# Turning the mLSTM score tiles over, with keys on partitions, in a two-block kernel on one core

## The chip, the cores and the metric

One Trainium2 chip, one of its cores. The program computes two blocks of two layers each in float32, from inputs in HBM to one output of 1024 by 256. The metric is the device time of one execution in microseconds. The time before is 2889.97 us, the median of three runs (2889.78 to 2895.23).

## The reference, cut to what matters

The change lies in the mLSTM half of the even layer of the second block. There are 512 tokens (256 of context, then 256 latents), 4 heads of 128 channels, and two directions. In each direction a latent sees the whole context, and within its own stream what lies behind it in that direction. With one chunk in place of the chunks of 64 the sum over keys reads:

```
b      = cumsum(log_sigmoid(forget gate))            per head and direction
dlog   = b[t] - b[s] + li[s]                         for the keys s that t may see
m[t]   = max(state's own exponent (0 to begin with, decayed), max over s of dlog)
dw     = exp(dlog - m[t])
sc     = (q[t] . k[s]) * dw
h[t]   = (sum over s of sc * v[s]) / max(|sum over s of sc|, exp(-m[t]))
ml     = rmsnorm(sigmoid(o) * (h_forward + h_backward)) * ml_norm_g
gla    = rmsnorm(o_gla) * gla_norm_g * silu(gla_g)
y      = concat(gla, ml) @ even_w_out
```

## The kernel before

Five instruction streams are written out by hand: SP (the DMA queue), TensorE, VectorE, ScalarE and GpSimd. They meet at named semaphores, so the order within a stream is the order in the code. An `InOrder` wrapper puts a drain behind most VectorE and ScalarE instructions. The four PSUM banks `accs` are handed round by the projections (`ready` and `free` per bank), and the four banks `mix` are the scratch of everything else.

The even layer projects 14 weight panels of 256 columns (`G["even"]`, panels u = 0 to 13). Each weight is split in two parts (`high` by ScalarE, `low` by GpSimd, line 1451) and each product takes three passes (lines 697 to 699, function `split_half`, for features on partitions; lines 742, 743 and 749, function `kept_tokens`, for tokens on partitions). Panels 2 and 3 (GLA values) and 10 and 11 (mLSTM values) are by token; 12 and 13 are the mLSTM output gate and by feature. Between the halves of the panels run the steps of the GLA tree: event e = 2u + r on each engine (`even_after` on TensorE and ScalarE, `even_event` on VectorE), up to `gla_cross` (line 1093) and `gla_out` (lines 1105 to 1110). Until then the stream of projections sets the time and the tree fills in.

Then comes the part that is changed:

- `ml_select` (line 1136), on TensorE: 32 matmuls that lay the eight rows `li - b` (four heads, two directions) out over all 128 partitions, one bank at a time, with ScalarE copying each bank to `rall` (`gla_heads`, line 1760).
- Panel 13 (`even_last`), with the mean square and the root of the GLA heads between its halves (`head_mean_square` line 1148, `head_spread` line 1155).
- `mlstm`, in four passes p over the query blocks t = 2, 3, 0, 1 of 128 tokens. Queries lie on the partitions, keys on the free axis. On VectorE `decays(p)` adds the row `rall`, the column b[t] and a causal mask for eight (head, direction) rows (line 2622), takes the maximum along the keys (line 101), and ScalarE takes the exponential (lines 1793, 1796). VectorE then multiplies by the scores and sums along the keys (line 2663), divides by the denominator (lines 2673, 2676), TensorE transposes (line 1180), ScalarE copies to SBUF, TensorE multiplies by the values (line 1189), ScalarE copies out (`ml_h`).
- Gate and head norm by feature: `half_squares`, `head_root`, `head_reciprocal`, `normalise` (line 2642), once for the latents and once for the context.
- `even_out`: the output projection, 4 panels of 16 fp32 matmuls of 512 columns (line 1202 for the first, line 682 for the other three). Each stands as two instructions in the trace, as every fp32 matmul does.

The panel queue on SP loads a panel when the one four places earlier has been read. At panel 10 it also loads four causal masks (line 619).

## Time and profile before

| | us |
|---|---|
| median of three runs | 2889.97 |
| the profiled execution | 2889.35 |
| its span | 2887.4 |
| TensorE matmul busy | 2676.5 (93%) |
| VectorE busy | 1944.3 (67%) |
| ScalarE busy | 1091.1 (38%) |
| GpSimd busy | 241.4 (8%) |
| the DMA queue's share of 16 engines | 44.5% |

Busy times are sums over the whole span; a stage can look quite different. TensorE's granted clock is given in each stretch: 1.00 is 2.4 GHz and 0.50 is 1.2 GHz, and values between are stretches that hold both. Where two matmul instructions follow each other their time is the distance of their starts, not the duration, since they overlap. The same goes for ScalarE and VectorE instructions without a drain.

### The profile page before, as it was taken

How to read it: one execution, taken by the hardware profiler on the slowest of the kernel's cores; microseconds unless marked ns; L12 is line 12 of the kernel's file. 1: busy time of each engine (PE TensorE's matmuls, PEld its weight loads, DVE VectorE, ACT ScalarE, POOL GpSimd, SP SyncE). 2: the span in 40 equal slices, each digit the busy share in tenths (PEclk: the TensorE clock that was granted, in tenths of full speed). 3: DMA queues.
4: the chain of work that ended last, by engine and by line, in shares of the span. 5: the costliest groups of instructions: out<-in, count | busy, mean ns of one | idle time of the engine just before them, and what ended most of it. 6: DMA issues, size and time to landing. Idle time of an engine off the chain costs nothing.

```text
span 2887.4 us, 48614 instructions
## 1 busy us (share of the span) xinstructions
PE 2676.5 (93%) x18294; PEld 2282.7 (79%) x18294; DVE 1944.3 (67%) x3306; ACT 1091.1 (38%) x1389; POOL 241.4 (8%) x135
## 2 busy tenths in 40 slices
PE   3999999999999989999989968999999899989998
PEld 3998988899998888899977854687744677768887
DVE  6776656777778666666746473577777767774781
ACT  2434432443543433254463552333300555542211
POOL 0000000000000000000013300244300000000100
PEclk9999999999999999999999989999999999999999
DMA  8775734677676553546412200222367221223442
GB/s 312 262 285 204 292 120 186 230 274 282 220 267 243 190 205 118 184 140 232 188 59 70 87 15 30 73 88 96 115 245 276 93 101 60 72 70 121 156 162 75
DMA packets 106384, 469.15 MB, mean 162 GB/s; under 512 B 7052, under 2 KB 57304, under 8 KB 58328
## 3 DMA queue, kind: packets, MB, share of 16 engines
q1 hardware_dynamic: 106200, 466.67, 44.5%
q8 instruction: 119, 1.95, 0.3%
q14 instruction: 65, 0.53, 0.1%
HBM read 465.58 MB, written 1.06 MB: 162 GB/s over the span
## 4 chain that ended last, share of the span: by engine, by line
PE 49%; DVE 24%; DVEq 8%; ACT 7%; DMA 6%; issue 4%; ACTq 1%; SPq 1%; POOLq 0%
PE accs L682 9%; PE accs L697 7%; PE accs L698 7%; PE accs L699 7%; DVE panel_r L86 4%; PE accs L834 4%; DMA panel<-w 3%; DVEq L2887 3%; DVE arena L2864 3%; ACT arena L76 2%; DVE arena L2163 2%; PE accs L1243 2%; DVE cond_panel L2163 2%; PE accs L1001 2%; PE accs L1244 1%
## 5 line engine op out<-in xcount | busy, mean ns | idle before, releaser
L697 PE MATMUL accs<-normed_r,arena_r 128*128 128x256 f32 (+2 forms) x1864 | 585.7, 314 | 17.5 <-DVEq L2208 7.2
L698 PE MATMUL accs<-arena_r 128*128 128x256 f32 x2069 | 584.4, 282 | 0.0
L699 PE MATMUL accs<-normed_r,panel_r 128*128 128x256 f32 (+2 forms) x1872 | 583.7, 312 | 0.0
L86 DVE TENSOR_TENSOR panel_r<-panel,arena_r 128x1024 fp32r<-128x1024 f32 (+1 forms) x295 | 390.1, 1323 | 162.2 <-ACTq L1523 117.0
L1522 ACT ACTIVATE arena_r<-panel 128x1024 fp32r<-128x1024 f32 (+1 forms) x292 | 330.5, 1132 | 383.6 <-DMA panel<-w 142.7
L697 PEld LDWEIGHTS accs<-normed_r,arena_r 128*128 128x128 f32 (+1 forms) x1864 | 350.5, 188 | 55.1 <-issue 12.7
L698 PEld LDWEIGHTS accs<-arena_r 128*128 128x128 f32 x2069 | 389.3, 188 | 1.1 <-issue 0.2
L699 PEld LDWEIGHTS accs<-normed_r,panel_r 128*128 128x128 f32 (+1 forms) x1872 | 350.1, 187 | 23.6
L682 PE MATMUL accs<-normed,panel 128*128 128x256 f32 x1536 | 341.0, 382 | 4.9 <-ACT normed L76 2.4
L2864 DVE SCALAR_TENSOR_TENSOR arena<-accs,vectors,arena 128x189 f32<-128x189 f32 (+2 forms) x704 | 279.2, 428 | 95.8 <-issue 64.7
L682 PEld LDWEIGHTS accs<-normed,panel 128*128 128x128 f32 x1536 | 289.6, 190 | 50.8 <-issue 4.1
L834 PE MATMUL accs<-arena,panel 128*128 128x256 f32 (+1 forms) x832 | 255.5, 469 | 1.6 <-DVEq L2769 0.8
L834 PEld LDWEIGHTS accs<-arena,panel 128*128 128x128 f32 x832 | 157.8, 190 | 98.8 <-issue 86.4
L76 ACT ACTIVATE arena<-accs 128x512 f32<-128x512 f32 (+2 forms) x128 | 75.3, 588 | 357.9 <-PE accs L699 232.4
L697 PE MATMUL accs<-arena_r 128*128 128x256 f32 x704 | 199.9, 284 | 9.6 <-DVEq L2208 9.5
L699 PE MATMUL accs<-arena_r,panel_r 128*128 128x256 f32 x704 | 198.3, 282 | 0.0
L1451 POOL TENSOR_TENSOR panel_r<-panel,arena_r 128x1024 fp32r<-128x1024 f32 x70 | 168.9, 2413 | 334.5 <-ACTq L1530 333.6
L1529 ACT ACTIVATE arena_r<-panel 128x1024 fp32r<-128x1024 f32 x72 | 76.3, 1060 | 205.0 <-PE accs L699 189.3
L76 ACT ACTIVATE arena<-residual 128x512 f32<-128x512 f32 (+1 forms) x56 | 31.9, 569 | 316.6 <-DVEq L2917 270.6
L91 DVE SCALAR_TENSOR_TENSOR residual<-accs,mods,residual 128x256 f32<-128x256 f32 x96 | 46.4, 483 | 150.2 <-PE accs L834 76.2
L697 PEld LDWEIGHTS accs<-arena_r 128*128 128x128 f32 x704 | 133.3, 189 | 11.9 <-issue 6.9
L699 PEld LDWEIGHTS accs<-arena_r,panel_r 128*128 128x128 f32 x704 | 133.1, 189 | 0.0
(425 smaller groups left out, 4630.9 us busy)
## 6 DMA issues: line engine op xcount, KB each, us to landing
panel<-w SPq DMA_DIRECT2D x250, 1024.0 KB, 4.9
panel<-w SPq DMA_DIRECT2D x48, 1408.0 KB, 8.1
cond_panel<-wc SPq DMA_DIRECT2D x57, 1024.0 KB, 6.2
normed<-wc SPq DMA_DIRECT2D x43, 1024.0 KB, 6.6
arena<-wc SPq DMA_DIRECT2D x19, 1024.0 KB, 5.4
residual<-xs SPq DMA_DIRECT2D x2, 1024.0 KB, 9.6
residual<-wc SPq DMA_DIRECT2D x1, 1024.0 KB, 13.1
residual<-crows SPq DMA_DIRECT2D x2, 512.0 KB, 9.2
```

The costliest lines, as they stand in the source:

```text
L76: i = self.eng.activation(*a, **k)
L86: i = self.eng.tensor_tensor(*a, **k)
L682: mm = pe.matmul(acc[b][:, o:o + ntok], w[:, k * PANEL + j * P:k * PANEL + j * P + P], rhs(k), start=(k == 0), stop=(k == KD - 1))
L697: pe.matmul(out, hi[:, k, 0:m], src_hi(k), start=clear and k == 0, stop=False, skip_group_check=True)
L698: pe.matmul(out, hi[:, k, 0:m], src_lo(k), start=False, stop=False, skip_group_check=True)
L699: mm = pe.matmul(out, lo[:, k, 0:m], src_hi(k), start=False, stop=last and k == n - 1, skip_group_check=True)
L834: mm = pe.matmul(acc[a % BANKS][:, o:o + ntok], w[:, k * PANEL + j * P:k * PANEL + j * P + P], src(part * kper + k), start=first, stop=(pa ...
L1451: pool.tensor_tensor(lo, half_panel(g, u, j), hi, ALU.subtract)
L1522: act.eng.activation(split_parts(g, u, j)[0], half_panel(g, u, j), ACT.Copy)
L2163: dve.eng.scalar_tensor_tensor(out=out, in0=wj, scalar=1.0, in1=row, op0=ALU.mult, op1=ALU.mult, accum_out=total)
L2864: dve.eng.scalar_tensor_tensor(out=out, in0=src, scalar=scale, in1=out, op0=ALU.mult, op1=ALU.add)
L2887: dve.drain()
```

## The change

Scores and decays get keys on the partitions and queries on the free axis. The exponent for a key s and a query t is (li[s] - b[s]) + (b[t] - m[t]); the first term is a column per key tile and becomes the bias of ScalarE's exponential, the second is a row that TensorE spreads over the partitions from a matrix of four rows.

- The maxima: ten pieces `ml_bounds(0..9)` on VectorE, on 4 and 36 partitions, in the events e = 10 to 19 (a scan for the forward direction, eight doubling steps for the backward one). Their rows come by four small DMAs at panel 7; the mask DMAs at panel 10 go.
- `ml_select` and the eight copies go. `ml_row(h, d)` is one matmul of 512 columns with 4 rows, two for each head.
- Panels 12 and 13 are projected by token (`kept_tokens`), and panel 13 is in the same loop as the others. The GLA mean square runs inside panel 13's first part, the spread between its parts.
- By head h = 0 to 3 and no longer by query block: ScalarE's exponentials (`ml_decays`, 8 per head, 2688 elements on the free axis in all), VectorE's mask by two predicated copies of four diagonal tiles, the products with the scores (7 instructions, 2688 elements), 20 matmuls of 129 columns with the decayed scores as weights and the values with a ones column behind them (`ml_heads`), and `finish`: denominators and reciprocal on 8 columns, four operations on 512 elements (two of them from PSUM), the last with the gate.
- No transposes of probabilities, no copies to SBUF of them, no accumulating reads. The norm is by token: ScalarE's squares with accumulation (4 per head), one root and one reciprocal for 16 columns, four multiplications (`ml_scaled`), then 16 transposes (4 per head) and four ScalarE copies into `ey`.
- `even_out` runs the GLA half of panel 0 ahead of the transposes and that of panel 1 behind them, then the mLSTM halves of both, then panels 2 and 3.

```diff
-        ML_ORDER = (2, 3, 0, 1)
+        ml_gate, ml_y, ml_tmp, ml_junk = region(E_Y + 2048, 4, 512), region(E_T + 4096, 4, 4, P), region(E_T + 6144, 4, P), region(E_T + 6656, 8, P)
+        brow, irow, mrow, crow = [t[0:36, KD * PANEL:KD * PANEL + 512] for t in slots]
@@ SP
-                        if g.name == "even" and i == 10:
+                        if g.name == "even" and i == 7:
                             sp.wait_ge(S("gla_sums"), 2)
-                            for n in range(4):
-                                sp.dma_start(mask_kept[n], io["consts"][:, m0 + n * T:m0 + (n + 1) * T]).then_inc(S("masks_loaded"), 16)
+                            sp.wait_ge(S("ml_rows"), 1)
+                            for d in range(2):
+                                sp.dma_start(brow[32 * d:32 * d + 4, :], cum16[8 * d + 4:8 * d + 8, :]).then_inc(S("masks_loaded"), 16)
+                                sp.dma_start(irow[32 * d:32 * d + 4, :], rows16[8 * d:8 * d + 4, :]).then_inc(S("masks_loaded"), 16)
@@ TensorE
+                elif e == 24:
+                    pe.wait_ge(S("ml_crow"), 1)
+                    even_evacuated(22, 24)
+                    for d in range(2):
+                        ml_row(0, d)
                 elif e == 25:
                     gla_out()
+                    pe.wait_ge(S("ml_exp"), 2)
+                elif e == 26:
+                    even_evacuated(24, 26)
+                    for d in range(2):
+                        ml_row(1, d)
+                    head_spread()
+            def ml_heads(h):
+                for t in range(4):
+                    q = slice(t * P, t * P + P)
+                    for d in range(2):
+                        keys = list(range(t + 1)) if d == 0 else list(range(t, 2)) if t < 2 else [0, 1] + list(range(t, 4))
+                        for s in keys:
+                            mm = pe.matmul(mix[:, t, d * (P + 1):(d + 1) * (P + 1)], ml_decay[h][:, d, s, q], mv[:, s, h, :],
+                                           start=(s == keys[0]), stop=(s == keys[-1]))
+                mm.then_inc(S("ml_av"), 1)
...
+                pe.wait_ge(S("ml_fin"), 2)
+                ml_heads(2)
+                pe.wait_ge(S("ml_p"), 12)
+                pe.wait_ge(S("ml_fin"), 3)
+                ml_heads(3)
@@ ScalarE
+            def ml_decays(h):
+                if h == 3:
+                    act.wait_ge(S("ml_av"), 1)
+                for d in range(2):
+                    act.wait_ge(S("ml_row"), 2 * h + d + 1)
+                    for s in range(4):
+                        t0, t1 = (s * P, 512) if d == 0 else ((0, 512), (0, 512), (T, T + P), (T, 512))[s]
+                        c = 8 * s + 4 * d + h
+                        act.eng.activation(ml_decay[h][:, d, s, t0:t1], ml_row_bank(h, d)[:, t0:t1], ACT.Exp, bias=dcol[:, c:c + 1])
+                    act.drain().then_inc(S("ml_exp"), 1)
@@ VectorE
+                def finish(h):
+                    dve.wait_ge(S("ml_av"), h + 1)
...
+                    dve.eng.tensor_tensor(ml_y[:, h, :, :], mix[:, :, 0:P], part[0], ALU.mult)
+                    dve.tensor_tensor(ml_tmp, mix[:, :, P + 1:2 * P + 1], part[1], ALU.mult).then_inc(S("ml_fin"), 1)
+                    dve.tensor_tensor(ml_y[:, h, :, :], ml_y[:, h, :, :], ml_tmp, ALU.add)
+                    dve.tensor_tensor(ml_y[:, h, :, :], ml_y[:, h, :, :], ml_gate[:, :, h * P:h * P + P], ALU.mult).then_inc(S("ml_gated"), 1)
...
+                products(0)
+                masks(1)
+                products(1)
+                finish(0)
+                masks(2)
+                products(2)
+                finish(1)
+                dve.tensor_tensor(ey[:, 0:4, :], go[:, :, :], ey[:, 0:4, :], ALU.mult).then_inc(S("ey_gla"), 1)
+                masks(3)
+                products(3)
+                finish(2)
+                finish(3)
+                dve.wait_ge(S("ml_std"), 1)
+                dve.reciprocal(ml_max[:, 16:32], ml_max[:, 0:16])
+                for h in range(4):
+                    dve.tensor_tensor(ml_y[:, h, :, :], ml_y[:, h, :, :], ml_max[:, 16 + 4 * h:20 + 4 * h].unsqueeze(2).to_broadcast([P, 4, P]), ALU.mult)\
+                       .then_inc(S("ml_scaled"), 1)
```

## Rows read from the trace of the kernel before

**Rows 1.** The page: the chain that ended last, share of the span by engine.
```profile
PE 49%; DVE 24%; DVEq 8%; ACT 7%; DMA 6%; issue 4%; ACTq 1%; SPq 1%; POOLq 0%
```

**Rows 2.** Stages: length, busy time (instructions) of each engine, granted clock, DMA share, GB/s.
```profile
1620.00:1664.90 44.90, 44.90 (x337) 41.16 (x336) 12.09 (x11) 21.19 (x22) 14.70 (x6) 1.00 0.20 71
1664.90:1708.50 43.60, 27.66 (x139) 19.33 (x137) 32.98 (x60) 28.84 (x52) 0.00 (x0) 0.88 0.07 25
1708.50:1757.70 49.20, 33.98 (x183) 28.89 (x184) 38.29 (x107) 17.41 (x29) 0.00 (x0) 0.79 0.00 1
1757.70:1776.00 18.30, 16.52 (x51) 7.71 (x50) 5.60 (x8) 3.16 (x6) 0.00 (x0) 1.00 0.00 0
1776.00:1818.00 42.00, 42.00 (x99) 18.62 (x98) 6.29 (x13) 3.77 (x6) 6.33 (x5) 1.00 0.22 75
```

**Rows 3.** The chain, 1620 to 1820: start us, us, what.
```profile
1628.25 0.31 PE accs L742
...
1665.44 7.16 PE accs L1136 x64
...
1679.11 1.00 PE mix L1148 x8
...
1776.25 41.21 PE accs L682 x96
```

**Rows 4.** TensorE in order of time: start us, us, line, operation, count.
```profile
1635.89 4.00 PE L749 MATMUL accs<-panel_r,normed_r 128*128 128x256 f32 x32
1639.82 3.73 PE L1093 MATMUL mix<-arena 64*128 64x256 f32 x32
...
1654.68 0.38 PE L1105 MATMUL mix<-arena 128*128 128x128 f32 x2
```

**Rows 5.** Groups by line and shape, 1672 to 1776: busy us, mean ns, idle before.
```profile
L1189 PE MATMUL mix<-arena 128*128 128x128 f32 x96 | 11.8, 280 | 0.2 <-ACT arena L76 0.2
L1793 ACT ACTIVATE normed<-normed,small 128x256 f32<-128x256 f32 x16 | 7.3, 495 | 0.1
...
L111 DVE RECIPROCAL std<-std 128x512 f32<-128x512 f32 x1 | 3.4, 3353 | 0.2 <-issue 0.2
...
L2652 DVE SCALAR_TENSOR_TENSOR arena<-arena,vectors,mix 128x512 f32<-128x512 f32 x4 | 2.7, 742 | 0.2 <-issue 0.2
...
L86 DVE TENSOR_TENSOR arena<-arena 128x2048 f32<-128x2048 f32 x1 | 2.3, 2291 | 0.1
...
L1767 ACT ACTIVATE arena<-mix 128x2048 f32<-128x2048 f32 x1 | 1.9, 1879 | 0.0
...
L2642 DVE SCALAR_TENSOR_TENSOR arena<-arena,vectors,mix 128x256 f32<-128x256 f32 x4 | 1.7, 477 | 3.1 <-PE mix L1155 3.1
```

**Rows 6.** In order of time: a root's table load, small operations, transposes.
```profile
1677.04 1.28 ACT L76 ACT_TABLE_LOAD   x1
...
1703.38 0.17 DVE L86 TENSOR_TENSOR small<-small 128x8 f32<-128x8 f32 x1
...
1726.09 3.39 PE L1180 MATMUL mix<-constants,arena 128*128 128x128 f32 x16 [6.91 <-DVEq L2678]
```

**Rows 7.** VectorE in the projections: end of one event, start of the next.
```profile
1579.26 0.75 DVE L2521 COPY_PREDICATED std<-constants,mix 128x512 f32<-128x512 uint32 x1 [0.17 <-issue]
1581.37 1.62 DVE L91 SCALAR_TENSOR_TENSOR arena<-accs,vectors,arena 128x510 f32<-128x510 f32 x2 [1.36 <-ACT arena L76]
```

**Rows 8.** Groups over the whole span: the scan, and ScalarE's accumulator read.
```profile
L106 DVE TENSOR_TENSOR_SCAN std<-arena 16x512 f32<-16x512 f32 x1 | 3.3, 3310 | 0.1
...
L76 ACT ACTIVATION_READ_ACCUMULATOR arena<-arena,small 128x1 f32 x16 | 3.0, 186 | 0.0
```

**Rows 9.** Short stretches in the columns of rows 2: TensorE's clock around its gaps.
```profile
1695.00:1700.00 5.00, 0.46 (x2) 0.00 (x0) 4.63 (x9) 4.59 (x13) 0.00 (x0) 0.83 0.01 2
...
1708.00:1712.00 4.00, 3.43 (x16) 3.46 (x17) 3.81 (x10) 0.00 (x0) 0.00 (x0) 0.50 0.00 0
1712.00:1716.00 4.00, 4.00 (x15) 2.09 (x14) 2.58 (x3) 1.88 (x1) 0.00 (x0) 1.00 0.02 6
```

More of the change, by code:

```diff
@@ new lines, in ml_row, with ml_score @@
+            def ml_row(h, d):
+                rows = slice(32 * d, 32 * d + 4)
+                pe.matmul(ml_row_bank(h, d), ident[rows, 32 * d + h:32 * d + h + 1].to_broadcast([4, P]), crow[rows, :], start=True, stop=True)\
+                  .then_inc(S("ml_row"), 1)
+            def ml_score(h, i):
+                out = ml_score_bank(h, i)
+                if i < 2:
+                    mm = pe.matmul(out, mqk[:, 4 + h, i * P:i * P + P], mqk[:, h, :], start=True, stop=True)
+                else:
+                    for s in range(2):
+                        mm = pe.matmul(out[:, s * T:s * T + T], mqk[:, 4 + h, T + s * P:T + s * P + P], mqk[:, h, T:2 * T], start=True, stop=True)
+                mm.then_inc(S("ml_scores"), 1)
@@ new lines, in mlstm @@
+            def mlstm():
+                pe.wait_ge(S("ml_exp"), 3)
+                ml_score(0, 0)
+                pe.wait_ge(S("ml_exp"), 4)
+                ml_score(0, 1)
+                even_evacuated(26, 27)
+                ml_score(0, 2)
+                even_evacuated(27, 28)
+                ml_score(1, 0)
+                pe.wait_ge(S("head_normed"), 1)
+                for t in range(4):
+                    mm = pe.transpose(mix[:, 3, 300 + 36 * t:336 + 36 * t], irow[:, t * P:t * P + P], ident[0:36, 0:36])
+                mm.then_inc(S("ml_ecol"), 1)
+                pe.wait_ge(S("ml_p"), 1)
+                ml_score(1, 1)
+                pe.wait_ge(S("ml_p"), 2)
+                ml_score(1, 2)
+                pe.wait_ge(S("ml_p"), 3)
+                ml_row(2, 0)
+                pe.wait_ge(S("ml_columns"), 1)
+                ml_heads(0)
+                pe.wait_ge(S("ml_p"), 4)
+                ml_row(2, 1)
+                pe.wait_ge(S("ml_p"), 5)
+                ml_score(2, 0)
+                pe.wait_ge(S("ml_p"), 6)
+                ml_score(2, 1)
+                pe.wait_ge(S("ml_exp"), 5)
+                ml_score(2, 2)
+                pe.wait_ge(S("ml_fin"), 1)
+                ml_heads(1)
+                pe.wait_ge(S("ml_exp"), 6)
+                ml_row(3, 0)
+                pe.wait_ge(S("ml_p"), 7)
+                ml_row(3, 1)
+                pe.wait_ge(S("ml_p"), 8)
+                ml_score(3, 0)
+                pe.wait_ge(S("ml_p"), 9)
+                ml_score(3, 1)
+                pe.wait_ge(S("ml_exp"), 7)
+                ml_score(3, 2)
+                pe.wait_ge(S("ml_fin"), 2)
[3 more added lines that the diff above has]
+                ml_heads(3)
@@ L1203, in part @@
                     return mm
                 pe.wait_ge(S("ey_gla"), 1)
[L1206 to L1215 removed]
+                for j in range(2):
+                    part(0, j, range(4))
@@ new lines, in even_out @@
+                for h in range(4):
+                    pe.wait_ge(S("ml_scaled"), h + 1)
+                    for t in range(4):
+                        mm = pe.transpose(mix[:, h, t * P:t * P + P], ml_y[:, h, t, :], ident)
+                    mm.then_inc(S("ml_turned"), 1)
+                for j in range(2):
+                    part(1, j, range(4))
+                for u in range(2):
+                    for j in range(2):
+                        part(u, j, range(4, KD), True).then_inc(ready[banks[u][j]], 1)
@@ L1216, in even_out @@
+                for u in range(2, 4):
                     features(g, 0, u, lambda k: ey[:, k, :], 512)
@@ L1405, in _ @@
                     even_gates()
-                    for u in range(13):
-                        if u in (2, 3, 10, 11):
+                    for u in range(14):
+                        if u in (2, 3, 10, 11, 12, 13):
                             kept_tokens(G["even"], u, even_after)
@@ L2638, in normalise @@
-                def normalise(n, tok):
-                    dve.wait_ge(S("head_bc"), n + 1)
-                    for h in range(4):
-                        dve.eng.scalar_tensor_tensor(out=ey[:, 4 + h, tok], in0=mqk[:, h, tok], scalar=col("ml_norm_g_2", h),
-                                                     in1=norm_spread[n][h], op0=ALU.mult, op1=ALU.mult)
-                    dve.drain().then_inc(S("head_normed"), 1)
-                decays(0)
-                head_reciprocal(0)
-                wait_ready(dve, G["even"], 0, 13, 1)
@@ L2649, in mlstm, with masks, weigh @@
-                decays(1)
+                def masks(h):
+                    dve.wait_ge(S("ml_exp"), 2 * h + 2)
+                    flat = decay_flat[h % 3]
+                    for d in range(2):
+                        near = flat[:, 1536 * d:1536 * d + 2560].rearrange("p (a b) -> p a b", a=4)[:, :, 512 * d:512 * d + P]
+                        dve.eng.copy_predicated(near, bc(outside[:, d * P:d * P + P].bitcast(mybir.dt.uint32), 4), bc(zeros, 4))
+                    dve.drain()
+                def weigh(h, d, s, t0, t1, piece):
+                    v = ml_decay[h][:, d, s, t0:t1]
+                    return dve.eng.scalar_tensor_tensor(out=v, in0=v, scalar=scale, in1=piece, op0=ALU.mult, op1=ALU.mult)
@@ L2650, in mlstm @@
+                dve.wait_ge(S("head_std"), 1)
+                dve.reciprocal(g_std, g_std).then_inc(S("head_rec"), 1)
+                masks(0)
                 dve.wait_ge(S("head_bc"), 1)
```

335 lines of the change are left out of this document (133 added, 202 removed).

## The prediction

> **What bounds the kernel now.** I first read the chain that ended last: TensorE 49% of it, VectorE 24% [rows 1]. An average says nothing about one stage, so I next cut the stretch around the change into windows [rows 2]. The reader is to see three kinds. Up to 1665 the projections keep TensorE busy for 44.90 of 44.90 us, VectorE only for 12.1. From 1665 to 1758 it is the other way: TensorE is busy for 61.6 of 92.8 us, VectorE for 71.3, and what VectorE does between two bursts of TensorE sets the time. From 1758 on TensorE is the bound again, with the output projection, whose last instruction ends at 1776.25 + 41.21 = 1817.5 [rows 3]. So a saving in the two middle windows counts in full, if nothing else is late there; before and after them only TensorE's own instructions count. GpSimd and the DMA queue are idle in the middle (DMA share 0.07 and 0.00) and can't be what comes next.
>
> **The change part by part.** I walk along the path, in the times of the trace of before, and ask when that last matmul ends.
>
> *Panels 12 and 13, up to the first score.* Panel 12 starts where `gla_cross` ends, 1639.82 + 3.73 = 1643.55 [rows 4]. By token a panel costs 1635.89 - 1628.25 = 7.64 for its first part [rows 3, 4] and 3.93 for the second [rows 4]. An fp32 matmul of 512 columns is two instructions at 41.21 / 96 = 0.429 us, so 0.86 [rows 3]; I price `ml_row` so too, though it has only 4 rows of weights (bounds: half of that, and 1.2). Then: first part 1651.2, two rows 1652.9, second part 1656.8, `gla_out` (1665.44 - 1654.68 = 10.76 [rows 3, 4]) 1667.6, three quarters of panel 13's first part 1673.3, mean square 1.0 [rows 3] 1674.3, last quarter 1676.2, two rows 1677.9. The spread waits for ScalarE's root (0.7 by the slope of [rows 5]) and VectorE's reciprocal of 3.35 [rows 5]: 1674.3 + 0.1 + 0.7 + 0.1 + 3.35 = 1678.6. TensorE waits there for 0.7, spreads in 3.4 and ends the second part of panel 13 at 1686.1. The 7.16 us of `ml_select` [rows 3] are paid back here by four rows, the longer panels and that wait, so this part gains next to nothing by itself; what it gains is that scores can start at once.
>
> What hides the rest of it: VectorE copies `go` from PSUM (2.29, as 2048 elements in [rows 5]) and ScalarE squares it (1.88 [rows 5]) by 1672.1, before TensorE asks at 1673.3, and the root's table load (1.28 [rows 6]) ends by 1673.4. The exponentials of head 0 run under `gla_out`, those of head 1 under the spread.
>
> *`ml_bounds`, events 10 to 19.* VectorE stands idle for 1.36 us between one event's predicated copy and the next event's convolution tap [rows 7]; the eight doubling steps cost at most 0.7 plus a drain each, which fits. The first piece holds a scan; the only fp32 scan of 512 elements took 3.31 [rows 8]. The last piece holds seven operations, some 4.4 us at 0.6 to 0.7 each, 3 more than the gap. Queued behind it are VectorE's step 15 of the tree and the sums that ScalarE waits for; TensorE asks for them one event later and panels 10 and 11 stand between. I take 0 on the path; if TensorE waits for both, it is 2 + 3 = 5 us. The four DMAs at panel 7 come in place of four larger ones at panel 10; their data is ready since event 4, and the panel loads behind them have an event of lead. 0, at most 2.
>
> *The heads.* VectorE, per head: products of 2688 elements in 7 instructions. From 2.7 / 4 = 0.68 at 512 and 1.7 / 4 = 0.42 at 256 elements [rows 5] an element costs 1.0 ns and an instruction 0.15: 3.7, with three drains 4.1. Masks: two predicated copies of 512 at 0.75 [rows 7], 1.6 with the drain. `finish`: three operations on 8 columns, 0.17 [rows 6] and some 0.25 apart, 0.8; two on 512 from PSUM, 1.4; two more, 1.5; together 3.7. In all 9.4 per head, and 2.3 once for `ey`. TensorE, per head: two rows 1.7, scores 2.6, 20 matmuls of 129 columns at two instructions of 11.8 / 96 = 0.123 or less [rows 5], 4.7: 9.0. ScalarE: the exponentials cost 0.5 at 256 and about 0.77 us per thousand elements beyond [rows 5], less an overlap of 0.1: 3.8, squares 4 x (0.3 + 0.19 [rows 8]), less overlap 1.6: 5.4. So VectorE and TensorE are near even and take turns.
>
> Going through the waits one by one (0.1 us for each crossing): scores of head 0 from 1686.1 to 1688.8; products(0) to 1691.2, masks(1) 1692.9, products(1) 1697.0; `ml_heads(0)`, held by `ml_p` 3 and two scores, 1693.0 to 1697.7; finish(0) 1697.8 to 1701.5. masks(2), products(2), finish(1) and `ey` fill VectorE without a gap to 1713.3, masks(3) and products(3) to 1719.0, and `ml_fin` 3 comes at 1721.2. TensorE has ended `ml_heads(2)` at 1715.1 and is idle for 6.1 us. `ml_heads(3)` is 4.7 at 2.4 GHz. Before, after such a gap (TensorE idle from 1695.5) the clock stood at 0.50 for the 4 us after the restart and at 1.00 in the next [rows 9]: 1.8 us are lost. Ends 1727.8.
>
> *Norm and output projection.* While VectorE finishes head 3 (to 1731.6), ScalarE squares and takes the root (1733.7) and VectorE multiplies (1734.8 to 1737.1), TensorE has the first GLA half of the projection, 6.9 us, to 1734.7. Transposes: 3.39 / 16 = 0.21 at the low clock [rows 6], so 0.85 a head at most; the last follows `ml_scaled` 4 and ends at 1737.7. Waiting in all 2 us. The rest of the projection is 112 instructions x 0.429 = 48.1, so the end is 1785.8. Removed with it: the accumulating reads, the tile divisions, 48 transposes, and two rounds of root, reciprocal and spread.
>
> **Sum.** 1817.5 - 1785.8 = 31.7 us. Nothing behind reads a different tile, the panel queue is four panels ahead (DMA share 0.22 in the projection [rows 2]), so it counts in full. The profiled execution's own time is 2889.35 (span 2887.4 and 1.95 around it), 0.6 below the median: 2889.35 - 31.7 = 2857.7.
>
> **The clock, row and rule.** In the two middle windows the granted clock was 0.88 and 0.79 [rows 2]; it fell after TensorE had stood idle and came back under work [rows 9]. The Trainium skill says the same in other words ("TensorE: Matmul & The Clock Gate", Part 1: the throttled state is the default, and activity releases it), and it warns of a kernel whose bursts are broken by waits and which starts each burst at the low clock. By that rule the finer hand-over between engines speaks against this change; it is rivals 2 and 3, worked out from rows.
>
> **The rivals.**
> 1. *Shorter (chance 0.16).* `ml_row` at half the price, VectorE's pieces nearer to 0.6 per 512, no dip: 4 heads x 1 + 1.7 + 1.8 + 1.5 = 9 less, 2849. For it: accumulating reads are gone. Against: the drains stay.
> 2. *A dip at every head (0.16).* Each gap costs a restart at half rate, 1.8 us, at three more heads, and VectorE's waits grow: 2857.7 + 5 to 9 = 2865. For it: before, the gap of 6.9 us ahead of the transposes at 1726.09 brought one too, 0.21 each [rows 6]. Against: TensorE has 9.0 us of work in each 9.4.
> 3. *Slower (0.04).* The clock stays at 1.2 GHz from the first score through the first panel of the projection. TensorE's 33 us of rows, scores and heads become 66 and end at 1752.8 in place of 1727.8, 2 us of VectorE behind them, and the first panel costs 13.75 more: the end is 1825.5, 8 late, 2897. It decides once more than 32 us of TensorE work are doubled. Against: before, the clock came back within 4 us of work, and at 1757.7 to 1776 it was 1.00 [rows 2, 9].
> 4. *The tree is delayed (0.10).* `ml_bounds` on VectorE's queue holds `gla_x` in events 10 to 20: 2857.7 + 5 to 7 = 2863.
> 5. *The chain is as long as before (0.03).* An unseen wait between ScalarE's exponentials and VectorE's masks at each head, 8 us x 4: no change, 2889.
>
> **How the numbers follow.** The forecast, with 2852 to 2863 as its own spread, has 0.51. The range takes in rivals 1, 2 and 4: 2846 to 2870. Left out are 3, 5 and the tails of 1 and 2. A difference of 0.2%, 5.8 us, is about what can be told from none. Faster: 0.51 + 0.16 + 0.16 + 0.10 = 0.93, same 0.03, slower 0.04.
>
> **What would show it.** The mLSTM windows together (from 1665 to the first `even_out` matmul) should shrink from 92.8 to about 62, with VectorE idle for under 8 us between the first product and the last `finish`. The last projection matmul ends near 1786. `ml_heads` takes 4.7 us at a clock of 1.00, its fourth time longer. The projections up to 1643.5 stay where they are. What would make the prediction wrong: predicated copies or products with broadcast operands slower than [rows 5, 7], a clock under 0.8 from 1686 to 1728, or TensorE idle in events 10 to 21.

## The result, and the profile after

The changed kernel takes 2858.39 us (median of three runs, 2857.95 to 2861.58) against 2889.97; the ratio is 0.9893 with a 95% interval of 0.9879 to 0.9906. The forecast was 2857.7, in 2846 to 2870. The profiled execution of the changed kernel took 2861.58 (span 2859.8), the upper end of its three runs, while that of the kernel before was 0.6 below its median. So the total fits better than the steps do, and the steps are what follows. A second profile of the same kernel, `after_again`, is compared with it below.

The chain that ended last, from 1600 to 1800 (columns as in [rows 3]):

```profile
1625.84 2.66 DVE arena L2580
...
1683.60 5.40 PE mix L1159 x8
...
1726.90 6.89 PE mix L1185 x40
...
1743.23 20.60 PE accs L1247 x48
1763.83 27.48 PE accs L687 x64
```

The last matmul of the projection ends at 1763.83 + 27.48 = 1791.3, where [rows 3] gave 1817.5: 26.2 us earlier. Behind it both profiles are alike (2887.4 - 1817.5 = 1069.9 and 2859.8 - 1791.3 = 1068.5), so the gain lies in this stage, as the sum had it. Three of the lines are longer than the forecast has them, and each becomes an experiment: an addition of `arena` at 2.66 us, the spread at 5.40, and the heads' matmuls at 6.89.

TensorE in order of time, from the first score to the projection. The last column is the idle time before and what ended it:

```profile
1692.66 1.88 PE L1172 MATMUL accs<-arena 128*128 128x512 f32 x4
...
1699.52 4.73 PE L1185 MATMUL mix<-arena,decay_sums 128*128 128x129 f32 x40
1704.19 1.12 PE L1165 MATMUL accs<-panel,constants 4*128 4x512 f32 x2
1705.24 1.98 PE L1172 MATMUL accs<-arena 128*128 128x512 f32 x4
1707.06 1.03 PE L1175 MATMUL accs<-arena 128*128 128x256 f32 x4
1707.92 4.63 PE L1185 MATMUL mix<-arena 128*128 128x129 f32 x40
...
1716.52 4.63 PE L1185 MATMUL mix<-arena,normed 128*128 128x129 f32 x40
1726.90 6.88 PE L1185 MATMUL mix<-arena,decay_sums 128*128 128x129 f32 x40 [5.76 <-DVE arena L86]
1733.62 7.03 PE L1247 MATMUL accs<-arena,panel 128*128 128x512 f32 x16
```

Line 1185 is `ml_heads`, 1165 `ml_row`, 1172 and 1175 the scores, 1247 the first panels of the projection. Up to 1721 TensorE has no gap; then it waits 5.76 us for VectorE, and the fourth `ml_heads` is slow. The windows of the same stretch (columns as in [rows 2]):

```profile
1657.00:1692.60 35.60, 34.55 (x233) 28.46 (x233) 9.71 (x8) 17.90 (x27) 4.78 (x2) 0.95 0.09 30
1692.60:1721.20 28.60, 28.52 (x166) 20.61 (x165) 23.72 (x43) 16.76 (x40) 0.00 (x0) 1.00 0.11 38
1721.20:1733.60 12.40, 6.70 (x40) 6.73 (x41) 6.35 (x14) 1.28 (x8) 0.00 (x0) 0.72 0.00 0
1733.60:1750.00 16.40, 16.14 (x51) 7.81 (x50) 6.24 (x12) 4.53 (x14) 0.00 (x0) 1.00 0.00 1
```

The first column behind the length is TensorE, the third VectorE. Where [rows 2] showed TensorE busy for 33.98 of 49.20 us at a clock of 0.79, it is now busy for 28.52 of 28.60 at 1.00, beside VectorE's 23.72. What remains of the old picture is one stretch of 12.4 us, at 0.72.

### The profile page after: what moved, and what is told of

It reads as the page before. It is cut to its first block, busy times and chain, and to the rows that moved or that the text cites. A ratio compares the mean times of both kernels' runs of the same rounds, so it can differ in the third digit from the quotient of the medians.

```text
span 2859.8 us, 48632 instructions
## 1 busy us (share of the span) xinstructions
PE 2674.9 (94%) x18346; PEld 2282.1 (80%) x18346; DVE 1931.4 (68%) x3229; ACT 1078.2 (38%) x1387; POOL 240.4 (8%) x135
## 3 DMA queue, kind: packets, MB, share of 16 engines
HBM read 465.05 MB, written 1.06 MB: 163 GB/s over the span
## 4 chain that ended last, share of the span: by engine, by line
PE 49%; DVE 24%; DVEq 9%; ACT 7%; issue 5%; DMA 5%; ACTq 1%; SPq 1%; POOLq 0%
PE accs L702 7%; PE accs L703 7%; PE accs L704 7%; PE accs L687 7%; DVE panel_r L86 4%; DVEq L2951 4%; PE accs L842 4%; DVE arena L2928 3%; DMA panel<-w 2%; ACT arena L76 2%; DVE arena L2209 2%; DVE arena L86 2%; PE accs L1291 2%; PE accs L1009 2%; DVE cond_panel L2209 2%
## 5 line engine op out<-in xcount | busy, mean ns | idle before, releaser
L702 PE MATMUL accs<-normed_r,arena_r 128*128 128x256 f32 (+1 forms) x1832 | 573.8, 313 | 16.6 <-DVEq L2254 7.3
L704 PE MATMUL accs<-normed_r,panel_r 128*128 128x256 f32 (+1 forms) x1840 | 572.1, 311 | 0.0
L702 PEld LDWEIGHTS accs<-normed_r,arena_r 128*128 128x128 f32 x1832 | 345.1, 188 | 52.3 <-issue 13.2
L704 PEld LDWEIGHTS accs<-normed_r,panel_r 128*128 128x128 f32 x1840 | 344.9, 187 | 22.3
L76 ACT ACTIVATE arena<-residual 128x512 f32<-128x512 f32 (+1 forms) x56 | 31.9, 569 | 307.9 <-DVEq L2981 261.9
```

The costliest lines, as they stand in the source:

```text
L76: i = self.eng.activation(*a, **k)
L702: pe.matmul(out, hi[:, k, 0:m], src_hi(k), start=clear and k == 0, stop=False, skip_group_check=True)
L704: mm = pe.matmul(out, lo[:, k, 0:m], src_hi(k), start=False, stop=last and k == n - 1, skip_group_check=True)
```

## Experiments

All kernels were timed beside the kernel before. Executions of one and the same kernel differ by up to 8 us (`after_again`, the changed kernel once more: 2852.37 to 2860.69) and once by 11 (`all_three`: 2844.47 to 2855.58), as much as most edits here are worth. So apart from the ratios I compare lengths within the profiles, between three landmarks that every kernel has: the start of VectorE's scan of 16 rows ([rows 8], some 160 us ahead of the stage), the start of `gla_cross` on TensorE, and the end of the last matmul of the projection.

| kernel | scan to gla_cross | gla_cross to end | both | median us | ratio, 95% |
|---|---|---|---|---|---|
| before | 161.13 | 177.63 | 338.76 | 2889.97 | |
| changed | 164.94 | 145.73 | 310.67 | 2858.39 | 0.9879 to 0.9906 |
| changed, again | 164.72 | 144.72 | 309.44 | 2859.49 | 0.9866 to 0.9899 |
| bounds_late | 161.05 | 145.59 | 306.64 | 2854.25 | 0.9856 to 0.9889 |
| ey_in_gap | 164.98 | 143.13 | 308.11 | 2857.20 | 0.9870 to 0.9903 |
| spread_late | 164.51 | 144.62 | 309.13 | 2856.92 | 0.9863 to 0.9896 |
| filler | 164.77 | 143.46 | 308.23 | 2855.29 | 0.9858 to 0.9891 |
| no_masks | 164.97 | 143.00 | 307.97 | 2856.94 | 0.9860 to 0.9893 |
| scores_behind | 164.76 | 155.29 | 320.05 | 2870.76 | 0.9919 to 0.9952 |
| before_no_maxima | 161.62 | 174.55 | 336.17 | 2886.34 | 0.9980 to 0.9999 |
| no_max_scores_first | 162.76 | 172.30 | 335.06 | 2883.27 | 0.9970 to 0.9989 |
| all_three | 160.97 | 141.58 | 302.55 | 2853.43 | 0.9843 to 0.9882 |
| all_four | 161.37 | 140.75 | 302.12 | 2854.87 | 0.9864 to 0.9897 |
| all_four_short | 162.33 | 139.95 | 302.28 | 2852.24 | 0.9855 to 0.9888 |

The changed kernel has two profiles; its mean is 145.2 from `gla_cross` to the end and 310.05 for both. They lie 1.0 and 1.2 apart, so against the mean a difference under about 1 us is not told from none. Ahead of `gla_cross` the four kernels that are alike there (bounds_late, all_three and the two all_four) differ by 1.4.

`after_again` repeats what was expected of it: TensorE waits 2.04 us for VectorE ahead of the tree's step 15, and the fourth `ml_heads` starts at a clock of 0.50. But it also shows where its 1.0 us comes from. The spread (line 1159) waits 1.05 us in both profiles; it then takes 5.40 in the first and 3.70 in the second. The fourth `ml_heads` waits 5.76 and 5.74, and takes 6.88 and 7.59. So 1.7 us less stand against 0.7 more. The short spread is also in one of the experiments, scores_behind:

```profile
1683.55 3.70 PE L1159 MATMUL mix<-std,constants 128*128 128x512 f32 x8 [1.05 <-DVE std L111]
```

The other four that have the spread in the same place (bounds_late, ey_in_gap, filler, no_masks) took 5.31 to 5.40, behind the same wait. Which of the two comes is not explained by any run. For these four I therefore also give the difference to the first profile (145.73), and for scores_behind that to the second (144.72).

### The bounds and the tree: bounds_late

```diff
-                if 10 <= e <= 19:
-                    ml_bounds(e - 10)
+                if 10 <= e <= 18 or e == 22:
+                    ml_bounds(min(e - 10, 9))
```

> The last piece of the maxima (`ml_bounds(9)`, 3.8 us of VectorE) is moved from event 19 to event 22, where VectorE had nothing to do from 1638.4 to 1649.3. Theory (the piece holds tree step 15, TensorE waits 2.0 us for it and then runs the first part of panel 11 partly at 1.2 GHz, 1.5 us): 3.5 us less than the changed kernel, 2855, no TensorE wait in events 10 to 21 and a clock of 1.00 there. Rival (VectorE's two multiplications of step 15 are slow, 2.66 and 2.85 us, because GpSimd runs beside them, and would be so wherever they stand): the wait stays, 0 to 1 us less.

Measured: 161.05 from the scan to `gla_cross`, 3.8 less than in the changed kernel and the same as before. The changed kernel shows how the last piece costs that much. VectorE first, then GpSimd, then TensorE, in order of time:

```profile
1624.99 0.68 DVE L86 TENSOR_TENSOR panel<-panel 36x512 f32<-36x512 f32 x1
1625.84 2.66 DVE L2580 TENSOR_TENSOR arena<-arena 128x512 f32<-128x512 f32 x1 [0.17 <-issue]
1628.42 2.85 DVE L2581 TENSOR_TENSOR arena<-arena 128x512 f32<-128x512 f32 x1
```

```profile
1625.45 2.50 POOL L1498 TENSOR_TENSOR panel_r<-panel,arena_r 128x1024 fp32r<-128x1024 f32 x1 [6.67 <-ACTq L1577]
1628.12 2.59 POOL L1498 TENSOR_TENSOR panel_r<-panel,arena_r 128x1024 fp32r<-128x1024 f32 x1 [0.18 <-issue]
```

```profile
1631.35 1.16 PE L1089 MATMUL mix<-arena 64*128 64x128 f32 x16 [2.02 <-DVEq L2582]
```

`ml_bounds(9)` itself takes from 1622.06 to 1625.67, 3.6 us, of which the idle gap took up a part. But it pushes the two additions of the tree's step 15 (lines 2580 and 2581) behind the start of GpSimd's two subtractions. They take 2.66 and 2.85 in place of 0.69 and 0.68. The ends tell why: GpSimd's end at 1627.95 and 1630.71, VectorE's 0.55 and 0.56 later, at 1628.50 and 1631.27. As I read these ends, VectorE stood still until GpSimd was through and then did its work. In the kernel before, one such operation of 2.87 stood at 1626.31; now there are two in a row. TensorE waits 2.02 for them, and then the granted clock is 0.66 from 1631.3 to 1635 and 0.86 to 1638, which with the wait makes the 3.8. In bounds_late only one addition meets GpSimd, TensorE doesn't wait, and the clock is 1.00 there. Behind `gla_cross` nothing changes (145.59 for 145.73). So the theory held. Of its rival, that the two additions are slow wherever they stand, one half is left: the second is still slow, but TensorE doesn't wait for it.

```profile
1624.47 0.69 DVE L2580 TENSOR_TENSOR arena<-arena 128x512 f32<-128x512 f32 x1 [1.28 <-ACT arena L76]
1625.08 2.87 DVE L2581 TENSOR_TENSOR arena<-arena 128x512 f32<-128x512 f32 x1
```

The Trainium skill ("SBUF — State Buffer", Who interferes with whom) says that a VectorE instruction with two inputs in SBUF contends with a GpSimd instruction that reads SBUF, and that one of them blocks for the whole of the other. The ends above agree with it: VectorE's lies 0.55 and 0.56 behind GpSimd's. GpSimd's second subtraction, begun 0.38 us before VectorE's first addition ended, took 2.59 where the one at 1616.39 took 2.40.

### The late spread: spread_late

The call of `head_spread()` moves from event 26 to event 27, behind the second part of panel 13.

> Only the spread of the GLA norm is moved, from ahead of the second part of panel 13 to behind it. In the changed kernel TensorE waited 1.05 us for the reciprocal and then ran the spread at a clock of 0.51, 5.40 us where 3.4 were forecast. Theory: wait and dip go, TensorE reaches the first scores 3 us earlier, but VectorE gets the spread only 0.8 us later than now and is the next bound, so the first product starts some 1 us earlier and the time falls by 1 us (0.5 to 1.5). Rival (TensorE alone sets the pace up to 1721, where it is busy all the time): 3 us less.

Measured: 144.6, so 0.1 to 1.1 less than the two profiles of the changed kernel; not told from none. The step itself did what was expected. The changed kernel first, spread_late second:

```profile
1683.60 5.40 PE L1159 MATMUL mix<-std,constants 128*128 128x512 f32 x8 [1.05 <-DVE std L111]
```

```profile
1687.26 3.59 PE L1160 MATMUL mix<-std,constants 128*128 128x512 f32 x8
```

The wait of 1.05 and the time of 5.40, at a clock of 0.51 and then 0.82, are gone: 3.59 at 1.00. Where these 2.9 us went, the three profiles show. From `gla_cross` to the start of `ml_heads(0)` it is 52.22 us here, 53.95 in the first profile and 52.26 in the second, which had the wait but not the dip. So the dip's 1.7 arrive there and the wait's 1.05 doesn't: TensorE is at its first score 1.1 us earlier than in the second profile, but VectorE's multiplication with the late spread (1690.89, 2.73 us) now ends just ahead of the first product (1693.74), and TensorE waits for that one. Of the 1.7, 0.6 are lost again at the fourth head, which takes 7.51 here and 6.88 in the first profile.

### The gap ahead of the fourth head: ey_in_gap and filler

ey_in_gap moves VectorE's multiplication `ey[:, 0:4] = go * ey` (2.29 us) from ahead of `masks(3)` to between `finish(2)` and `finish(3)`, where VectorE waits for TensorE in any case.

> The multiplication of the GLA half into `ey` (2.29 us of VectorE) is moved from ahead of masks(3) to between finish(2) and finish(3), where VectorE stood idle 5.5 us. Theory (from head 1 on VectorE's queue sets the time, with TensorE idle 5.8 us ahead of `ml_heads(3)`): the products of head 3 end 2.3 us earlier, the gap falls to 3.5 us, and the time by 2.3 (the dip of the clock stays) to 4.4 us (it goes too): 2854 to 2856. Rival (TensorE and VectorE bound alternately and TensorE is full up to 1721): 0 to 1 us.

Measured: 143.1, 2.1 less than the mean and 2.6 less than the profile with the same long spread; 2.3 to 4.4 was the theory, 0 to 1 the rival. TensorE, in ey_in_gap:

```profile
1722.34 6.16 PE L1185 MATMUL mix<-arena,decay_sums 128*128 128x129 f32 x40 [3.88 <-DVE arena L86]
```

The wait fell from 5.76 to 3.88, by 1.9, and `ml_heads(3)` from 6.88 to 6.16, together the 2.6: a gap of 3.9 us still brings a dip of 1.5 (1.7 in all_three, with the same gap).

filler leaves the gap's length to VectorE, but fills it with 22 matmuls whose result nobody reads:

```diff
+                pe.wait_ge(S("ml_exp"), 8)
+                for _ in range(22):
+                    pe.matmul(ml_row_bank(3, 1)[:, 0:P], ident, ident, start=True, stop=True)
                 pe.wait_ge(S("ml_p"), 12)
```

> 22 fp32 matmuls of 128 columns without use (some 5 us) go into the gap of 5.8 us ahead of `ml_heads(3)`, in a bank that nobody reads. Theory (the gap itself makes the clock fall, and the fall costs 2.2 us of `ml_heads(3)`, 6.9 in place of 4.7): the clock stays at 1.00 there, `ml_heads(3)` takes 4.7, and the time falls by 2 us (1 to 2.5). Rival (the clock falls after something else, or the work behind it isn't on the path): no change, or later by what the filler overlaps, up to 0.5 us.

Measured: 143.5, 1.8 less than the mean and 2.3 less than the first profile, and the fourth head as fast as the others:

```profile
1718.63 5.08 PE L1235 MATMUL accs<-constants 128*128 128x128 f32 x44
1724.53 4.70 PE L1185 MATMUL mix<-arena,decay_sums 128*128 128x129 f32 x40 [0.82 <-DVE arena L86]
```

So the excess of `ml_heads(3)` over 4.7 us is the clock's, and it hangs on what TensorE did just before: in the changed kernel the clock was 0.50 from 1727 to 1730, and with the fillers it is 1.00 from 1724.5 to 1730. The Trainium skill ("TensorE: Matmul & The Clock Gate", Part 1) says that activity releases the throttle; these traces agree.

### Which engine binds up to the gap: no_masks

VectorE's two predicated copies of each head are left out, so the causal mask is missing from the result.

> The predicated copies of the diagonal tiles are left out (keys ahead of the query then count too, so the output is another one). They are 1.4 us of VectorE for each head; those of head 0 lie under a wait. Theory (VectorE's queue is on the path from head 1 on): 2 to 3 x 1.4 = 2.8 to 4.2 us less than the changed kernel, 2854 to 2855.5. Rival (TensorE is the bound for heads 0 to 2, where it was busy 28.4 of 28.4 us): only the copies of head 3 count, 1.4 us.

Measured: 143.0, 2.2 less than the mean and 2.7 less than the first profile, though VectorE has 5.4 us less to do (1.35 in each of four heads). That lies between the theory (2.8 to 4.2) and the rival (1.4). VectorE, in no_masks:

```profile
1705.66 0.17 DVE L86 TENSOR_TENSOR small<-mix,bias_causal 128x8 f32<-128x8 f32 x1 [2.87 <-PE mix L1185]
...
1713.95 0.17 DVE L86 TENSOR_TENSOR small<-mix,bias_causal 128x8 f32<-128x8 f32 x1 [0.77 <-PE mix L1185]
```

At the first `finish` VectorE now waits 2.87 for TensorE, where it waited 1.15, and 0.77 at the second, where it didn't wait. `ml_heads(2)` starts 70.95 us behind `gla_cross` with the masks and without, `ml_heads(3)` 81.33 with them and 79.24 without; the other 0.6 is its smaller dip (6.25). So up to `ml_heads(2)` the masks cost TensorE nothing; only those of the last heads are on the path.

### When the scores are issued: scores_behind

TensorE issues the scores of head h + 1 behind `ml_heads(h)` and no longer ahead of it.

> The changed kernel with one edit: TensorE issues the scores of head h+1 behind ml_heads(h) instead of ahead of it, as the kernel before had them behind the transposes. Nothing else moves. Theory (a good part of the gain is that scores lie ready in a bank of their own when VectorE comes): VectorE waits at the products of heads 1, 2 and 3 for the 4.7 us of ml_heads(h) in part and for the scores themselves, in all 6.5 to 10 us with the lower clock that follows; from the start of the scan to the end of the projection 317 to 320 us against 310, time 2865 to 2869. Rival (the order is free, because VectorE's or TensorE's own work sets the stage): 0 to 2 us.

Measured: 155.3, 10.1 more than the mean and 10.6 more than the profile with the same short spread, and 2870.76 us, 1.8 above the range that I expected. This one edit takes back more than a third of the 28.7 us (338.76 - 310.05) that the stage had gained. TensorE and VectorE, in order of time, in scores_behind:

```profile
1703.09 1.88 PE L1172 MATMUL accs<-arena 128*128 128x512 f32 x4
1704.81 1.03 PE L1175 MATMUL accs<-arena 128*128 128x256 f32 x4
1705.76 1.12 PE L1165 MATMUL accs<-panel,constants 4*128 4x512 f32 x2
1710.30 6.34 PE L1185 MATMUL mix<-arena 128*128 128x129 f32 x40 [3.42 <-DVE arena L86]
```

```profile
1704.15 1.22 DVE L2695 SCALAR_TENSOR_TENSOR arena<-arena,accs 128x1024 f32<-128x1024 f32 x1 [6.58 <-PE accs L1172]
...
1717.54 1.22 DVE L2695 SCALAR_TENSOR_TENSOR normed<-normed,accs 128x1024 f32<-128x1024 f32 x1 [4.40 <-PE accs L1172]
```

VectorE waits 6.58 and 4.40 for scores, and 2.01 at the last head; then TensorE waits 3.3 to 4.4 for VectorE, and every `ml_heads` takes 6.34 to 6.37 in place of 4.63. That is rival 2 of the prediction, a dip at every head, brought about by the order of two calls:

```profile
1707.00:1710.00 3.00, 0.00 (x0) 0.00 (x0) 2.58 (x9) 1.81 (x4) 0.00 (x0) 1.00 0.00 0
1710.00:1714.00 4.00, 3.70 (x18) 3.73 (x19) 2.88 (x5) 1.28 (x8) 0.00 (x0) 0.58 0.00 0
1714.00:1718.00 4.00, 4.00 (x28) 3.25 (x27) 0.46 (x1) 0.00 (x0) 0.00 (x0) 1.00 0.00 0
```

TensorE stands idle through the first window, works at a clock of 0.58 in the second and is back at 1.00 in the third. The other two thirds of the gain no run divides: how much the transposes, the divisions and the second round of the norm were worth is argued from the rows and not shown.

### Was it VectorE's work before: before_no_maxima and no_max_scores_first

before_no_maxima is the kernel before without the pass that adds rows, columns and masks (line 2622) and without the maxima; ScalarE takes the exponential of `rall` itself. Masks and maxima are missing from its result.

```diff
-                        dve.eng.scalar_tensor_tensor(out=dlog[:, i, o:o + T], in0=rall[:, i, o:o + T], scalar=bt[:, d, h:h + 1], in1=mask, op0=ALU.add, op1=ALU.add)
...
-                    dve.tensor_reduce(m, dlog[:, :, o:o + T], AXX, ALU.max)
+                    dve.tensor_copy(m, ml_max[:, 0:8])
```

> The kernel before, with its pass for the maxima left out: no addition of row, column and mask (line 2622) and no maximum along the keys (line 101) in the four query blocks; the exponential reads the spread rows directly, so the output is another one. VectorE loses 4 x (3.26 + 2.29) = 22.2 us. It asks how much of the change's gain could come from moving the maxima out of the way. Theory (all four lie on the path, the first partly beside ScalarE's copies): 18 to 22 us less than the kernel before, 2868 to 2872, two thirds of the gain of 31.6. Rival (they lie beside transposes, copies and scores, which would be waited for instead): under 12 us, 2878 or more.

Measured: 22.2 us of VectorE's work are gone, and the stage is 2.6 us shorter (336.17 against 338.76). VectorE and TensorE, in before_no_maxima:

```profile
1712.87 0.69 DVE L2658 SCALAR_TENSOR_TENSOR normed<-normed,accs 128x512 f32<-128x512 f32 x1 [7.33 <-PE accs L1162]
...
1728.75 0.42 DVE L2658 SCALAR_TENSOR_TENSOR arena<-arena,accs 128x256 f32<-128x256 f32 x1 [5.05 <-PE accs L1162]
```

```profile
1705.18 3.64 PE L1180 MATMUL mix<-constants,arena 128*128 128x128 f32 x16 [10.59 <-DVEq L2673]
1708.62 4.14 PE L1162 MATMUL accs<-arena 128*128 128x512 f32 x8
```

The freed time became waiting for scores. TensorE idles 10.59 for the probabilities, transposes them at half clock, and only then computes the next scores. So what the first paragraph of the prediction read off [rows 2], VectorE busy for 71.3 of 92.8 us, was true and still not what set the time. Of the four passes over the maxima the last two (11.1 us) lay inside the round trip from VectorE to the transposes to the scores and back, and became the waits of 7.33 and 5.05 (1.34 and 0.33 before). The first two lay ahead of the first product, beside panel 13: with them it stands 58.3 us behind `gla_cross`, without them 57.3, where it waits 2.61 for the first scores, which take 5.36 in place of 3.67.

no_max_scores_first issues the scores of pass p + 1 ahead of the transposes of pass p.

> As before_no_maxima (the kernel before without the maxima and the mask pass of a head: neither the 24 products with their masks nor the maximum are made, so the output is another), with one more edit: on TensorE the scores of head p+1 are issued ahead of the transposes of head p instead of behind them. Theory (what set the time of the stage before was the round trip VectorE, transposes, scores, VectorE and not VectorE's sum): VectorE's waits for the scores, 7.33, 5.05 and 1.68 us in before_no_maxima, shrink by about the 3.6, 3.5 and 1.1 us of transposes that stood ahead of the scores; from the start of the scan to the end of the projection about 329 us instead of 336.2, so some 6 to 8 us less, time about 2879. Rival (the transposes, their copies and the value matmuls behind them are as late as before and become the wait): 0 to 2 us less.

Measured: 172.3 from `gla_cross`, 2.3 less than before_no_maxima, and 1.1 less for both parts: the rival, not the 7 us. VectorE's wait at the second pass is still 6.18. The row on TensorE says why:

```profile
1708.92 6.43 PE L1162 MATMUL accs<-arena 128*128 128x512 f32 x8 [10.59 <-DVEq L2673]
```

The scores of the second pass still start 10.59 us after TensorE's last work, because the edit leaves them behind the wait for the probabilities (`ml_prob`), and now it is they that start at half clock (0.50 from 1708 to 1712), 6.43 in place of 4.14. At the third pass the wait did fall, from 5.05 to 1.65, and at the fourth VectorE then waited 2.28 for ScalarE's exponentials. So the place relative to the transposes is not what holds them; the wait is. How much of it the banks demand is less than that: VectorE's last product that reads them ends at 1703.4, and the divisions behind it, which no longer touch them, release the scores 5.5 us later. Whether scores released there, on the one set of banks, would have opened the round trip no run shows, and a second set of banks was not tried on the kernel before either.

### Together: all_three, all_four, all_four_short

all_three is bounds_late, spread_late and ey_in_gap in one; all_four adds the 22 fillers; all_four_short has 17.

> bounds_late and ey_in_gap together, and the spread of the GLA norm moved behind the second part of panel 13, so that the reciprocal (3.35 us) runs under that part. Theory: 3.5 + 2.3 to 4.4 + 1 to 3 us less than the changed kernel: 2847.5 to 2851.6. Rival (each saving uncovers the same next wait, so that they don't add up): 3 to 5 us less, 2853 to 2855.

> all_three (bounds of the last chunk later, spread matmuls later, the normalizer's multiplication later) with the 22 filler matmuls ahead of ml_heads(3) as well. The fillers compute nothing that is used. Theory (the remaining gap of some 3.9 us still costs the clock behind it): ml_heads(3) falls from 6.16 to about 4.7 us, 1 to 2 us less than all_three, so from the start of the scan to the end of the projection about 301 us against 302.6, time about 2852. Rival (the fillers of 5.1 us outlast the shorter gap and delay ml_heads(3)): 0 to 1 us more than all_three.

> all_four with 17 filler matmuls in place of 22. In all_four the fillers began at 1712.76 and lasted 5.08 us, to 1717.67, while VectorE's release of ml_heads(3) (the second 512-column operation of finish(2), 1715.99 + 0.68) came at 1716.7: a delay of 1.0 us. 17 take 5.08 x 34 / 44 = 3.9 us and would end as the release comes. Theory (the gain of 1.7 us at ml_heads(3) was partly eaten by this delay): ml_heads(3) still takes 4.6 to 4.7 us and starts 1.0 us earlier, from the start of the scan to the end of the projection about 301.1 us against 302.1. Rival (the last fillers are what keeps the clock up, or TensorE's end is not what ends the stage): 0 to 1 us more than all_four. The medians can't tell it; the stage can.

Measured: all_three saves 7.5 us of the stage (302.55 against 310.05) where the three alone save 3.4, 0.9 and 1.9. Against the first profile (310.67) the three save 4.0, 1.5 and 2.6, which is 8.1, and all_three saves 8.1: they add up, and by the stage it is the theory (6.8 to 10.9). By the median alone it would be the rival (2853 to 2855). It is 2853.43 us against the kernel before's 2891.02 beside it. Its upper end of 0.9882 lies under the changed kernel's 0.9893, though the two intervals overlap. all_four takes off only 0.8 behind `gla_cross`, between the two expectations, and its rows say how:

```profile
1712.76 5.08 PE L1236 MATMUL accs<-constants 128*128 128x128 f32 x44
1717.67 4.63 PE L1186 MATMUL mix<-arena,decay_sums 128*128 128x129 f32 x40
```

`ml_heads(3)` is down from 6.34 to 4.63, but VectorE had released it at 1716.7 and the fillers ran until 1717.67: 1.7 won, 1.0 lost. With 17 fillers:

```profile
1713.36 3.96 PE L1236 MATMUL accs<-constants 128*128 128x128 f32 x34
1717.41 4.70 PE L1186 MATMUL mix<-arena,decay_sums 128*128 128x129 f32 x40
```

It starts 0.15 after VectorE's release (1716.58 + 0.68 = 1717.26) and keeps its 4.70: the step went as the theory had it. Behind `gla_cross` that is 0.8 less again, 139.95; ahead of it the execution lost 1.0, so the sum of both stays at 302.3 and the whole is not told from all_three. Its median, 2852.24 us (ratio 0.9872), is the lowest of all kernels here, but all_three's ratio to the kernel before beside it is lower (0.9862), and no runs separate the two.

## Why the prediction was right, step by step

**What binds.** Wrong in its reason, right in its consequence. [rows 2] was read as VectorE's own work setting the time. before_no_maxima refutes that: 22.2 us less of it gave 2.6. What set the time was the round trip, in which VectorE's products and divisions are only a part and TensorE starts each transpose from idle; that a single set of score banks forced it is argued. The sum didn't rest on the reason, since it priced the new stage from its own operations and not the old one by what was taken away; a forecast by "VectorE's removed work" would have failed.

**The walk.** It starts from `gla_cross`, which began at 1645.57 in place of 1639.82; the measured times below are moved back by those 5.75.

| step | forecast | measured, moved |
|---|---|---|
| two rows, panel 12 | 1651.2 | 1651.2 |
| second part of panel 12 | 1652.9 | 1652.3 |
| `gla_out` | 1656.8 | 1656.2 |
| GLA mean square | 1673.3 | 1672.6 |
| spread | 1678.6 | 1677.9 |
| first score | 1686.1 | 1686.9 |
| `ml_heads(0)` | 1693.0 | 1693.8 |
| `ml_heads(3)` | 1721.2 | 1721.2 |
| first matmul of the projection | 1727.8 | 1727.9 |
| end of the projection | 1785.8 | 1785.6 |

From `gla_cross` on the gain is 177.63 - 145.73 = 31.9, the sum's 31.7. In detail terms cancel. Two `ml_row` together were cheaper than forecast:

```profile
1656.99 1.13 PE L1165 MATMUL accs<-panel,constants 4*128 4x512 f32 x4
```

That is two matmuls in some 1.06, for 1.7 forecast. But it is no lower price of one: where a single `ml_row` is issued it takes as long (1704.19 to 1705.24 above), more than the 0.86. The two of a pair read rows 0 to 3 and 32 to 35, and run side by side. The spread went the other way, 5.40 against 3.4, because a dip of the clock followed the wait ahead of it; the prediction had the wait (0.7, measured 1.05) but no dip, and in `after_again` there was none. On TensorE a head took 8.4 and 8.6 us (the starts of `ml_heads` above) where 9.0 was forecast: a single row or a pair for 1.05 in place of 1.7. VectorE's pieces, in order of time:

```profile
1719.39 1.35 DVE L2687 COPY_PREDICATED decay_sums<-bias_causal 128x512 f32<-128x512 uint32 x2
1720.82 1.22 DVE L2699 SCALAR_TENSOR_TENSOR decay_sums<-decay_sums,accs 128x1024 f32<-128x1024 f32 x1
1722.16 2.42 DVE L2693 SCALAR_TENSOR_TENSOR decay_sums<-decay_sums,accs 128x384 f32<-128x384 f32 x6
```

Masks 1.4 with the drain (forecast 1.6) and products 3.9 (4.1). "Near even and take turns" was right, as no_masks shows, and so was the fourth head's dip: 2.2 us for 1.8 (2.9 in `after_again`).

**What was given 0.** `ml_bounds` was taken at 0, with 5 us as the other bound and 0.10 for it as rival 4. Rival 4 is what happened, at 3.8 us for its 5 to 7; in bounds_late it is gone. The prediction compared the last piece, 4.4 us of work (measured 3.6), with the gap of 1.36 and saw the excess of 3, but then let panels 10 and 11 cover it. It missed that being late moves VectorE's additions onto GpSimd's subtractions. The row of 2.87 stood in the trace of before; it was not among the rows that I read. Forecast and rival 4 were no alternatives: both came true, one in each part of the stage.

**How the total came out.** From the forecast end of 1785.8 to the measured 1791.3 are 5.5 us: 3.8 for the bounds, 1.9 because this execution reached the scan 1.9 later (1480.63 against 1478.69; across the kernels here that point lies anywhere from 1475.8 to 1482.0), and -0.2 in the rest, in which the spread's dip of 1.7 us is paid for by the cheaper rows and VectorE's shorter pieces. The stretch behind, with the little around the span, gave back 1.6. That leaves 2861.6 for the profiled execution against 2857.7. That the median lies only 0.7 from the forecast is partly luck: the forecast lacked 3.8 us, and bounds_late, the kernel without them, has a median of 2854.25, 3.5 below it.

**The rivals.** 1 (shorter): a pair of `ml_row` came at 0.6 of its price and no lower, and the missing dip was wrong. 2 (a dip at every head): not here, but scores_behind shows that it was one call away, at 10.1 us, more than the 5 to 9 I gave it. 3 and 5: nothing of them; between 1692.6 and 1721.2 the clock was 1.00. **Signs that I named:** the middle was to shrink from 92.8 to about 62; counted from the same distance behind `gla_cross` (25.1 us) it is 1733.62 - 1670.67 = 62.95. VectorE was to be idle for under 8 us; it was 10.5 of the 43.8 us from 1693.7 to 1737.5, small gaps included. The projections were to stay where they are and TensorE not to be idle in events 10 to 21; both failed, by rival 4.

## What to carry to other kernels

When an engine is busy for most of a stage, ask first whether its work lies in a round trip: what it waits for next may stand behind its own last result, and then removing work only lengthens the wait. Issue the producer ahead of the consumer's follow-up, where it has a place of its own to write; here, with that place given, the order of two calls was worth 10 us. Look also at what the producer waits for: a new order behind the same wait gave 1 to 2 us. And price work that is moved into a gap by what it pushes and by what the pushed instruction then meets, not by its own length. And where two executions of one kernel differ, find the row that differs before an edit is read against either.

## What the hardware did that I had not expected

- An addition of 512 columns on VectorE that starts while GpSimd subtracts over 1024 columns ends 0.55 us after GpSimd does (2.66, 2.85 and 2.87 us in place of 0.69).
- A short wait can be enough for a dip, and need not be: behind the same 1.05 us idle the clock stood at 0.51 for the next 2.4 us in the first profile of the changed kernel and at 1.00 in the second, and the spread was long in five profiles and short in two. The 2.0 us idle ahead of step 15 cost 1.5 more behind them in each of the seven profiles that have them (14.2 us to `gla_cross`, 12.7 in bounds_late). 0.39 and 0.15 us of waiting between the scores of all_four left `ml_heads` at 4.73.
- Two fp32 matmuls of 512 columns with 4 rows of weights each, on rows 0 to 3 and 32 to 35, took 1.06 us together, and one of them alone 1.05. One with 128 rows took 0.86 in a long series (41.21 / 48).
